# Retention's keys and values turned by VectorE in 32 by 32 blocks and by the transfers' patterns, instead of by TensorE

## The reference

```python
proj = jnp.einsum('bld,de->ble', rmsnorm(x, g_norm), w_in)      # 1024 -> 10240 columns
u_p, z_p, q, k, v, z_r, gates = jnp.split(proj, IN_SPLITS, axis=-1)
qh, kh = rope(q ...), rope(k ...) * 256 ** -0.5                 # 4 heads of 256; values 4 heads of 512
scores = jnp.einsum('bhid,bhjd->bhij', q, k) * decay[None]
inner = jnp.einsum('bhij,bhjv->bhiv', scores, v)
s_new = gamma ** C * s + jnp.einsum('bhjd,bhjv->bhdv', k_dec, v)  # contracts over positions
```

## Time and profile before

| what | value |
|---|---|
| median of 3 runs | 2836.22 us (2836.0 to 2837.22) |
| the profiled execution | 2833.37 us |
| its span | 2831.6 us |
| TensorE, VectorE, ScalarE, GpSimd busy | 98%, 64%, 40%, 24% of the span |
| transfers | 552.80 MB, 281849 packets |
| granted TensorE clock over the span | 0.997 |

### The profile page before, as it was taken

How to read it: one execution, slowest core, us unless ns; L and a number is a source line. 1 busy time by engine, 2 the same in 40 slices (tenths; PEclk the granted TensorE clock), 3 DMA queues, 4 the chain that set the end, 5 groups by cost and what they waited for, 6 DMA issues and landing times.

```text
span 2831.6 us, 36714 instructions
## 1 busy us (share of the span) xinstructions
PE 2782.2 (98%) x13504; PEld 2249.1 (79%) x13504; DVE 1808.3 (64%) x2588; ACT 1126.4 (40%) x1901; POOL 684.8 (24%) x456
## 2 busy tenths in 40 slices
PE   6999999999999999999999999999999999999998
PEld 5888888888877777777777787877887888788876
DVE  8667566667555365655755566676677667766775
ACT  5444444444554444443434433333333333333332
POOL 5253433434332223425334330000000000000000
PEclk9999999999999999999999999999999999999999
DMA  4544444454564344453444458487648764876496
GB/s 144 197 146 155 173 147 158 156 179 145 180 223 153 113 156 162 147 186 125 163 154 154 165 200 307 141 278 289 246 145 283 289 239 150 283 290 234 153 340 261
DMA packets 281849, 552.80 MB, mean 195 GB/s; under 512 B 24216, under 2 KB 166872, under 8 KB 270527
## 3 DMA queue, kind: packets, MB, share of 16 engines
q1 hardware_dynamic: 266279, 541.73, 53.5%
q10 hardware_dynamic: 15168, 8.46, 1.0%
q0 software_dynamic: 224, 0.26, 0.0%
HBM read 375.59 MB, written 175.14 MB: 194 GB/s over the span
## 4 chain that ended last, share of the span: by engine, by line
PE 90%; DVE 4%; DMA 2%; issue 2%; ACT 1%; POOL 0%; ACTq 0%; SPq 0%; DVEq 0%; POOLq 0%
PE bank L1310 28%; PE bank L1312 28%; PE bank L1311 28%; PE bank L1360 2%; PE bank L1383 1%; PE bank L1502 1%; DMA raw<-in_w_branch_ret 1%; DVE w_lo L2173 1%; DVE xa_lo L2173 1%; DVE xs L2187 1%; PE bank L1632 1%; PE bank L1620 0%; PE bank L1610 0%; DMA x_d<-x_out 0%; DMA raw<-in_w_branch_pool 0%
## 5 line engine op out<-in xcount | busy, mean ns | idle before, releaser
L1310 PE MATMUL bank<-xa_hi,wa_hi 128*128 128x512 f32 x2240 | 888.8, 397 | 5.5 <-ACT part_s L1864 3.2
L1312 PE MATMUL bank<-xa_hi,wa_lo 128*128 128x512 f32 x2240 | 873.6, 390 | 0.0
L1311 PE MATMUL bank<-xa_lo,wa_hi 128*128 128x512 f32 x2240 | 873.5, 390 | 0.0
L1310 PEld LDWEIGHTS bank<-xa_hi,wa_hi 128*128 128x128 f32 x2240 | 420.6, 188 | 107.8 <-issue 21.5
L1312 PEld LDWEIGHTS bank<-xa_hi,wa_lo 128*128 128x128 f32 x2240 | 420.5, 188 | 90.0
L1311 PEld LDWEIGHTS bank<-xa_lo,wa_hi 128*128 128x128 f32 x2240 | 421.1, 188 | 82.8
L2173 DVE TENSOR_TENSOR wa_lo<-w_raw,wa_hi 128x512 fp32r<-128x512 f32 x320 | 312.7, 978 | 165.9 <-ACT wa_hi L1857 165.1
L2173 DVE TENSOR_TENSOR wa_lo<-w_sum,wa_hi 128x512 fp32r<-128x512 f32 x240 | 194.2, 809 | 241.3 <-ACT wa_hi L1857 241.3
L2173 DVE TENSOR_TENSOR w_lo<-raw,w_hi 128x512 fp32r<-128x512 f32 (+1 forms) x288 | 181.9, 659 | 189.3 <-ACT w_hi L1971 189.2
L1857 ACT ACTIVATE wa_hi<-w_raw 128x512 fp32r<-128x512 f32 x320 | 201.2, 629 | 242.6 <-PE bank L1312 238.3
L1971 ACT ACTIVATE w_hi<-raw 128x512 fp32r<-128x512 f32 (+1 forms) x288 | 166.4, 603 | 306.6 <-PE bank L1312 208.5
(11 more groups left out here) (253 smaller groups left out, 4311.8 us busy)
## 6 DMA issues: line engine op xcount, KB each, us to landing
w_raw<-in_w_in SPq DMA_DIRECT2D x80, 1024.0 KB, 5.3
v_d<-turned SPq DMA_DIRECT2D x64, 512.0 KB, 3.2
qk_s<-qk_d SPq DMA_DIRECT2D x32, 1024.0 KB, 7.4
v_s<-v_d SPq DMA_DIRECT2D x32, 1024.0 KB, 11.5
raw<-in_w_branch_ret SPq DMA_DIRECT2D x128, 256.0 KB, 4.2
tabs<-in_c_rope SPq DMA_DIRECT2D x16, 1024.0 KB, 6.9
qk_d<-high SPq DMA_DIRECT2D x32, 512.0 KB, 4.6
qk_d<-c_low SPq DMA_DIRECT2D x32, 512.0 KB, 5.4
```

What stands on the lines that cost most here:

```text
L1310: pe.matmul(out, lh, rh, start=first, stop=False, skip_group_check=onto)
L1311: pe.matmul(out, lh, rl, start=False, stop=False, skip_group_check=onto)
L1312: return pe.matmul(out, ll, rh, start=False, stop=last, skip_group_check=onto)
```

## The change

VectorE turns the tiles within SBUF in blocks of 32 by 32, and what is left of the turn (which block goes where) is done by the access patterns of the transfers to and from DRAM. To that end a job's columns stand in another order: value jobs read their weight columns in strips of 32 (`weight_columns`), and the scratch tensors in DRAM have other shapes. A turned quarter is now stored by four transfers (one for each 32 partitions), in pieces of 256 B for keys and 512 B for values. The rotated queries and keys are stored as rows of 2 KB, four transfers per block of 512 positions instead of two; those of a key job are issued ahead of the second and the fourth turned quarter. Keys come back in two transfers a chunk instead of one.

TensorE's `turn` is removed, and with it the two banks' waits. VectorE's new `turn_blocks` runs in the first two slots of the following job, for keys into the space of the rope tables, for values in place; `turn_high` and `turn_low` read SBUF instead of PSUM. `rope_low` of a key job moves from slots 3 and 5 to 2 and 4, ahead of `turn_low`. In slot 0 `turn_blocks` stands ahead of the rope of the second 512 positions, in slot 1 behind it. The final states leave in four transfers a head instead of one.

```diff
+BT = 32
+BA = P // BT
-        turned = at("turned", [P, TURNED, 2, 2, DK], F32R)
+        turned = at("turned", [P, TURNED, 8, 2, 2, BT], F32R)
-            v_s.append(at(f"v_s{s}", [P, NC, 2, 2, DV], F32R))
+            v_s.append(at(f"v_s{s}", [P, NC, 2, 2 * BA, 2, 2 * BT], F32R))
-        qk_d = scratch("qk_d", [NB, HEADS, 2, P, 2, 2, T])
-        kt_d = scratch("kt_d", [NB, HEADS, NC, P, 2, 2, DK])
-        v_d = scratch("v_d", [NB, HEADS, NC, P, 2, 2, DV])
+        qk_d = scratch("qk_d", [NB, HEADS, 2, 2, 2 * P, T])
+        kt_d = scratch("kt_d", [NB, HEADS, BT, T // BT, 2, BA, 2 * BT])
+        v_d = scratch("v_d", [NB, HEADS, NT, P, 2, BA, 4 * BT])
...
         def tab_free(engine, j):
+                if kind(i) == "k":
+                    engine.wait_ge(turn_lo, 4 * before(i + 1, "k", "v"))
         def stores(j):
-            return {"q": 64, "k": 64, "v": 0}.get(kind(j), 32)
+            return {"q": 128, "k": 128, "v": 0}.get(kind(j), 32)
         def c_free(engine, j):
-                engine.wait_ge(turn_mm, 4 * before(j - 1, "k", "v"))
+                engine.wait_ge(turn_lo, 4 * before(j - 1, "k", "v"))
+        def weight_columns(j, rows, e):
+            w = w_raw[:, j % 2, rows, :]
+            if kind(j) == "v":
+                return w.rearrange("p k (a e s) -> p k a e s", a=BA, e=2)[:, :, :, e, :]
+            return w[:, :, e * P:(e + 1) * P]
+        def blocks(j, t, e):
+            if kind(j) == "v":
+                return c_out[:, j % 2, t, e, :]
+            return tabs[:, :, t * T:(t + 1) * T].rearrange("p c (b e s) -> p e c b s", b=8, e=2)[:, e]
...
+            def rotated(j, t):
+                what, i, _part = JOBS[j]
+                b = 2 * (j // NJ) + t
+                sp.wait_ge(qk_lo_done, 2 * before(j, "q", "k") + t + 1)
+                dst = qk_d[b, i, "qk".index(what)]
+                for low, src in enumerate((qk_high[t], c_low[:, j % 2, t])):
+                    for e in range(2):
+                        sp.dma_start(dst[low].rearrange("(a e s) t -> e a s t", a=BA, e=2)[e],
+                                     src[:, e, :].bitcast(F32)).then_inc(c_stored[j % 2], 16)
             def store(j):
                         sp.wait_ge(turn_lo, n + 1)
-                        dst = kt_d[b, i, c] if what == "k" else v_d[b, i, c][:, :, :, part * DK:(part + 1) * DK]
-                        sp.dma_start(dst, turned[:, n % TURNED].bitcast(F32)).then_inc(t_stored[n % TURNED], 16)
+                        if what == "k" and c:
+                            rotated(j, q // 2)
+                        for a in range(BA):
+                            src = turned[a * BT:(a + 1) * BT, n % TURNED].bitcast(F32)
+                            if what == "v":
+                                dst = v_d[b, i, 2 * c:2 * c + 2, :, part, a].rearrange("n (b r) x -> r (n b) x", b=BA)
+                                sp.dma_start(dst, src.rearrange("r b h e s -> r b (h e s)"))\
+                                    .then_inc(t_stored[n % TURNED], 16)
+                                continue
+                            dst = kt_d[b, i, :, 8 * c:8 * c + 8, :, a, :].rearrange("r b h x -> r (b h) x")
+                            sp.dma_start(dst, src.rearrange("r b h e s -> r (b h) (e s)")).then_inc(t_stored[n % TURNED], 16)
+                    if what == "q":
+                        rotated(j, t)
+            def keys_of_chunk(s, b, h, c):
+                for i in range(2):
+                    src = kt_d[b, h, :, 8 * c + 4 * i:8 * c + 4 * i + 4].rearrange("r b h a x -> b r (h a x)")
+                    sp.dma_start(kt_s[s][:, c, i].bitcast(F32).rearrange("p h d -> p (h d)"), src)\
+                        .then_inc(tv_arrived[s][c], 16)
...
-            def turn(j, q):
...
             def turn_high(j, q):
-                act.wait_ge(turn_mm, n + 1)
-                act.activation(turned[:, n % TURNED, 0].rearrange("p i d -> p (i d)"), banks[6 + q % 2][:], ACT.Copy,
-                               scale=turn_scale(j)).then_inc(turn_hi, 1)
+                act.wait_ge(blocks_turned, n - q + 2 * (q // 2) + 2)
+                act.activation(turned_part(j, n, 0), turned_source(j, q), ACT.Copy, scale=turn_scale(j)).then_inc(turn_hi, 1)
+            def turn_blocks(j, t):
...
+                for e in range(2):
+                    src = c_out[:, j % 2, t, e, :]
+                    if kind(j) == "k":
+                        src = src.rearrange("p (c b s) -> p c b s", c=2, s=BT)
+                    dve.transpose(blocks(j, t, e), src).then_inc(blocks_turned, 1)
...
                 for i in range(PROD):
                     evict(j, i)
+                    if j and kind(j - 1) == "k" and i in (2, 4):
+                        rope_low(j - 1, i // 2 - 1)
                     if j and kind(j - 1) in ("k", "v") and 2 <= i < 6:
                         turn_low(j - 1, i - 2)
                     weight_low(PROD * j + i + SLOTS)
+                    if j and kind(j - 1) in ("k", "v") and i == 0:
+                        turn_blocks(j - 1, 0)
                     if j and kind(j - 1) in ("q", "k") and i < 2:
                         rope(j - 1, 1, (i,))
+                    if j and kind(j - 1) in ("k", "v") and i == 1:
+                        turn_blocks(j - 1, 1)
```

More of the change, by code:

```diff
@@ L1116, in _ @@
                 if p < 4:
-                    sp.dma_start(io["ret_prompt"][0, 0, p].rearrange("(k p) v -> p k v", p=P), state[:, p])\
-                        .then_inc(state_stored, 16)
+                    final = io["ret_prompt"][0, 0, p].rearrange("(e k a s) v -> a e s k v", e=2, k=2, a=2)
+                    for part in range(BA):
+                        sp.dma_start(final[part // 2, part % 2], state[part * BT:(part + 1) * BT, p]).then_inc(state_stored, 16)
                 if p == 0:
@@ L1197, in weight_sums @@
             def weight_sums(j, steps):
-                b11, b12 = w_raw[:, j % 2, 0:KH, 0:P], w_raw[:, j % 2, 0:KH, P:2 * P]
-                b21, b22 = w_raw[:, j % 2, KH:KT, 0:P], w_raw[:, j % 2, KH:KT, P:2 * P]
+                b11, b12 = (weight_columns(j, slice(0, KH), e) for e in range(2))
+                b21, b22 = (weight_columns(j, slice(KH, KT), e) for e in range(2))
+                sums = [like_weights(j, w_sum[:, k]) for k in range(2)]
                 if 0 in steps:
@@ L1397, in _ @@
                         one_product(j, i)
-                    if j and kind(j - 1) in ("k", "v") and 1 <= i < 5:
-                        turn(j - 1, i - 1)
                     for k in range(PROD):
@@ L1489, in output @@
                         k = slice(j * CHUNK + t * P, j * CHUNK + (t + 1) * P)
-                        mm = split_product(out, sc_hi[:, c, k], sc_lo[:, c, k], v_s[s][:, c, 0, j, :],
-                                           v_s[s][:, c, 1, j, :], not cross and j == 0, j == t)
+                        mm = split_product(out, sc_hi[:, c, k], sc_lo[:, c, k], v_s[s][:, c, j, :, 0, :],
+                                           v_s[s][:, c, j, :, 1, :], not cross and j == 0, j == t)
                     mm.then_inc(o_mm, 1)
@@ L1582, in project_by_tiles @@
                     sample_head(b, 2 * KT + KT + KH + i)
-            pe.wait_ge(turn_lo, 4 * before(ALL, "k", "v"))
             rides_copied(pe, ALL)
@@ L2229, in weight_low @@
                 if i in (S1T1, S2T2, A22T4):
-                    src = w_sum[:, {S1T1: 0, S2T2: 1, A22T4: 1}[i]]
+                    src = like_weights(j, w_sum[:, {S1T1: 0, S2T2: 1, A22T4: 1}[i]])
                 else:
-                    src = {A11B11: w_raw[:, j % 2, 0:KH, 0:P], A12B21: w_raw[:, j % 2, KH:KT, 0:P],
-                           S3T3: w_raw[:, j % 2, 0:KH, P:2 * P], S4B22: w_raw[:, j % 2, KH:KT, P:2 * P]}[i]
-                tt(wa_lo[:, n % SLOTS], src, wa_hi[:, n % SLOTS].bitcast(F32), ALU.subtract, wa_lo_done)
+                    rows = slice(0, KH) if i in (A11B11, S3T3) else slice(KH, KT)
+                    src = weight_columns(j, rows, int(i in (S3T3, S4B22)))
+                tt(like_weights(j, wa_lo[:, n % SLOTS]), src, like_weights(j, wa_hi[:, n % SLOTS]).bitcast(F32),
+                   ALU.subtract, wa_lo_done)
             def tile(j, t, e):
@@ L2367, in _ @@
                             windows(j - 1, 1, i - 3, i - 2 if i < PROD - 1 else GROUPS + 1)
-                    for t in range(2):
-                        if j and (kind(j - 1), i) in (("q", 2 + 2 * t), ("k", 3 + 2 * t)):
-                            rope_low(j - 1, t)
+                    if j and kind(j - 1) == "q" and i in (2, 4):
+                        rope_low(j - 1, i // 2 - 1)
                     if kind(j) in ("q", "k") and i >= S4B22:
```

113 lines of the change are left out of this document (54 added, 59 removed).

## The result

The changed kernel takes 3157.15 us (median of 4 runs, 3156.83 to 3160.06) against 2836.56 us for the kernel before beside it: a ratio of 1.1132, 95% interval 1.1113 to 1.1152. It is slower, as forecast, but by 321 us instead of 124. The profiled execution has a span of 3155.0 us, 323.4 more than before. Where the time came from is worked out from two places in each trace, ScalarE's copy of the first product of the last projection job, and the end: the projection became 199.8 us longer (1667.7 to 1867.5), the rest 123.7 us.

A forecast was written before the change was run, and what follows sets the result against it. TensorE, busy 98% of the span, was taken to bound the kernel. Removed transposes -46.5, store waits +140, clock +14 and second stage +16 gave +123.5, so 2960 us against the median 2836.2; range 2860 to 3020.

The forecast's parts named there:

- the two long waits in the projection: Key and zp jobs: VectorE's first eviction waits for rotated stores to land; 5.8 and 11.7 us a first-half head.
- Removed, -46.5: Projection: 384 transposes leave TensorE, about 5.8 us a head over eight heads, all on the path.
- Block transposes, 0.60 each: VectorE, slots 0 and 1: four 32 by 32 block transposes a job, 2.4 us, up to 4.7.
- A22T4 1.3 us late behind S3T3: Value jobs after key jobs: the seventh product waits for VectorE's delayed eviction of S3T3, in 8 jobs.
- the further 1.6 us at S3T3: Key and zp jobs: VectorE's work queued ahead of S3T3's eviction adds 1.6 us after each long wait.
- Four engines: Rotated stores, 4 blocks outermost in DRAM, use 4 of 16 engines; forecast given 0.78.
- One rotated half (four transfers, 1 MiB) takes 10.3 us on 4 engines: Stores behind key and query jobs: 25 GB/s an engine, against 2.6 us on 16 engines.
- two more key lots of 1.3 to 1.6 us: Transfers behind a key job: turned-key stores between the two rotated halves, which run to 25.8 and 39.3 us.
- Clock, 14 within 0 to 27: After eight zp waits TensorE runs partly at 1.2 instead of 2.4 GHz, 1.7 us each.
- I take 1 us a head, 16 us; bounds 0 and 116: Second stage: key loads on 4 engines take 7.7 us more a head, raw weights behind them, mostly hidden.
- slower still: Rival: 4 engines, and the second stage pays most of its 7.7 us a head; 3044 us, chance 0.05.
- Spread over 16 engines: The faster rival: rotated lots use all 16 engines, only VectorE's 10 us delay remains; 2800 us, chance 0.13.

The follow-up runs named there:

- natural: both16 with the earlier kernel's scratch rows and channel order, rotated parts stored as 128 rows, key weights every second column; 2836.11 us, 0.9993 of the kernel before.
- both16: Changed kernel with rotated stores and turned-key loads both in transfers by strips of 32 partitions; 2852.86 us, 1.0059 of the kernel before.
- before4: Kernel before with a gap after each 32 scratch rows of rotated queries and keys, loads in four strips; 3103.10 us, 1.0940 of the kernel before.
- permuted: natural with each block of 32 holding every fourth position, so one load writes all 128 partitions; 2831.55 us, 0.9981 of the kernel before.
- keys16: Changed kernel with a chunk's turned keys loaded in four transfers of 32 partitions instead of two; 3073.03 us, 1.0841 of the kernel before.
- late_blocks: permuted with VectorE transposing a key job's second 512 positions only in slot 4, quarters and rotated issues moved; 2805.08 us, 0.9882 of the kernel before.
- permuted_shift: permuted with VectorE's low parts of a key job's quarters one slot later (3 to 6); 2823.47 us, 0.9952 of the kernel before.

## Why the prediction was wrong

The sign, the two long waits in the projection and the engine count were right; two terms of the sum were too small, the transfers' time in the projection and the second stage's, so that the time lies 137 us above the range.

- *Removed, -46.5:* right. Jobs that carried turns are as long as the others wherever nothing else is late (natural's key jobs 19.04 and 20.31).
- *Block transposes, 0.60 each:* right; 1.30 for two in a row, 0.69 as one row. A22T4 1.3 us late behind S3T3 in value jobs: its gap is 0.9 in both16, and the job 1.4 longer. (The 0.97 us of VectorE's idle time that the working put down to the turn on TensorE ends with ScalarE's copy in the earlier trace rows.) That the zp job has the same gap (1.1 in both16) was missed. In the changed kernel the further 1.6 us at S3T3, which the key and zp jobs were to lose behind their long wait, do not show.
- *Four engines:* right, and shown by the packets and by before4.
- *"One rotated half (four transfers, 1 MiB) takes 10.3 us on 4 engines":* this is the first step that failed; the engines were right, the time was too short. A packet of 2 KB took 94 ns in the first half behind a key job and 104 in the second, not the 82 behind 25 GB/s: 12.1 and 13.3 us on four engines. Other packets go between them: the first half's run from 17.3 to 31.1 us into the value job, the second's from 35.0 to 49.7, for 15.5 to 25.8 and 29 to 39.3 by my working. Of the 10.4 us by which the last packet is late, 7.9 lie in the two halves' own time, 1.8 in the first one's start and 0.7 between them. The second half landed at 50.3, for 40, and the queries land 2.5 us later in their job than by my working. In the head above, key jobs became 9.1 us longer, not 5.8, zp jobs 21.1, not 11.7; over all heads the projection lost 246 us to waits and clock, not 154.
- *"two more key lots of 1.3 to 1.6 us", issues at 0.32 to 0.43 us:* too small as well, with less effect. A key lot in pieces of 256 B is 2048 x 25.3 ns / 16 = 3.2 us of the engines' time; I had priced it from the old transfer of 512 KB in pieces of 4 KB. Issues of turned keys took 1.12 us in the median, so that SP came to the second half 33.4 us into the value job; most of this ran beside the first half's landing. What holds SP's issues back (a limit on what may be outstanding, or on one engine's share) is open; with spread stores they are short again.
- *Clock, 14 within 0 to 27:* 30. Each zp job loses 1.75 us, as priced, and each key job 2.0, which had no term.
- *Second stage, "I take 1 us a head, 16 us; bounds 0 and 116":* the second step that failed, and the larger miss against its term: 123.7. I took the middle stage's one wait of 2.5 us as room. But at a change of block the engines are full already (1.04 in the kernel before), and there the raw weights stand behind what a new head loads, and slower keys are paid in full: against permuted, whose loads have the same rows on 16 engines and all partitions, 123.7 - 7.5 = 116 us, 7.3 a head, for the 7.7 that I had as a bound, though TensorE pays it in stops of some 12 us about twice a block, with the clock behind them, and not at each head. The rival "slower still" had this mechanism, at 0.05, and its 3044 lacked the projection's other 90 us. keys16 gives 92 of it back, with strips in the place of four engines.
- *Spread over 16 engines, "1.3 x 8 = 10" is what is left:* this rival had no term for the second stage. In the kernels whose key loads go by strips, 27 to 38 us are still lost there.

The faster rival (spread, 2800) names what both edits should have given; both16 shows that spreading in strips gives 2853, and late_blocks that it takes whole transfers and a place for VectorE's transposes to reach 2805.

## What to carry to other kernels

Before a layout is changed, write down for each transfer the outermost count of both sides and the partitions that one transfer touches, and price it by those, not by its bytes: here 4 blocks outermost cost 215 us in one stage and 92 in the other (against strips), and strips of 32 partitions another 31. When such a transfer shares a queue with loads for the engine that binds, look for the windows in which the queue is full: there its whole extra time is paid, however few waits the stage shows. A permutation can be moved to where it is cheap: here into TensorE's weight pattern, for 2 us, instead of the stores, where it cost 14. And a wait of the binding engine can cost more than its length: behind a gap of 2.07 us in permuted the clock fell and cost 1.6 us more, behind one of 1.45 us in permuted_shift it did not.

## Not expected

- Where transfers that write 32 partitions are among the traffic, full engines move 298 and 261 GB/s; where the operands' loads write 128, 406 to 411.
- SP's issues of turned keys take 0.32 us each before, 1.12 in the median behind transfers on four engines (up to 5.84), and 0.54 once these are spread.
- A 32 by 32 block transpose of 128x512 takes 0.69 us with neighbouring columns and 1.09 with every fourth; a matmul whose weights are read with a stride of two takes 5 ns more, 394 for 389.
